# Layer C of a fused transformer kernel: softmax weights scaled and turned by one product with a diagonal, compressed keys on a block diagonal

## What is computed

```python
kc = compress(k_cmp, pe_k, wk1, wk2)          # 31 keys per group
vc = compress(v_cmp, pe_v, wv1, wv2)
# per block of 128 queries
s_c = einsum('bqghd,bngd->bghqn', qb, kc) * scale
p_c = masked_softmax(s_c, cmp_end[None, :] <= t[:, None])
o_c = einsum('bghqn,bngd->bqghd', p_c, vc)
p_s = masked_softmax(s_s, valid_s)            # selected keys
p_w = masked_softmax(s_w, valid_w)            # window keys
out = gb[..., 0:1] * o_c + gb[..., 1:2] * o_s + gb[..., 2:3] * o_w
```

## Time and profile before

| | us |
|---|---|
| median of 3 runs | 2537.54 (2537.01 to 2543.62) |
| the profiled execution, its own time | 2534.34 |
| its span in the trace | 2533.0 |
| layer C's attention in it: first logits to last values | 946.72 to 1156.83, 210.11 |
| PE busy over the span | 2307.1 (91%) |
| DVE busy | 1427.5 (56%) |
| ACT busy | 539.9 (21%) |

### The profile page before, as it was taken

The page is one execution under the profiler, slowest core; times in us unless marked ns, Lnnn a source line. Parts: engine busy times, 40 slices in busy tenths (PEclk is TensorE's granted clock), DMA queues, the critical chain, the costliest instruction groups (busy, mean ns, idle before and its releaser), DMA issues.

```text
span 2533.0 us, 29573 instructions
## 1 busy us (share of the span) xinstructions
PE 2307.1 (91%) x10920; PEld 1680.7 (66%) x10920; DVE 1427.5 (56%) x3707; ACT 539.9 (21%) x1325; POOL 65.9 (3%) x67
## 2 busy tenths in 40 slices
PE   8997889999999978889999999998889688988887
PEld 6864578888888864547888888885566533333332
DVE  6559867656656538887666566664756411111114
ACT  2013342101002015542110011103454211111111
POOL 0000000000000000000000000000000011111110
PEclk9998799999999968999999999998699899999999
DMA  5212002232224300001322223222003499999996
GB/s 206 91 50 67 1 18 84 84 93 91 84 83 153 99 18 1 1 1 51 92 92 83 83 91 93 84 84 87 1 1 135 169 357 419 419 419 419 419 420 289
DMA packets 69455, 350.18 MB, mean 138 GB/s; under 512 B 10804, under 2 KB 11060, under 8 KB 43776
## 3 DMA queue, kind: packets, MB, share of 16 engines
q1 hardware_dynamic: 64144, 339.18, 36.2%
q0 software_dynamic: 4880, 8.05, 0.9%
q10 hardware_dynamic: 288, 1.05, 0.1%
HBM read 343.05 MB, written 17.30 MB: 142 GB/s over the span
## 4 chain that ended last, share of the span: by engine, by line
PE 66%; DVE 9%; DMA 7%; ACT 3%; issue 2%; SPq 0%; DVEq 0%; POOLq 0%
PE bank L549 24%; PE bank L562 7%; PE bank L552 7%; PE bank L557 7%; PE bank L2253 6%; DMA w<-in_experts 6%; PE bank L2261 4%; PE bank L540 2%; DVE exps L1678 1%; PE bank L751 1%; DVE exps L1849 1%; PE bank L2229 1%; DMA y_pairs<-oN,idx 1%; PE bank L821 1%; PE bank L971 1%
## 5 line engine op out<-in xcount | busy, mean ns | idle before, releaser
L2253 PE MATMUL bank<-w,xT 128*64 128x512 f32 x1024 | 230.5, 598 | 9.1 <-DMA w<-in_experts 8.4
L2416 DVE COPY square<-bank 128x256 f32<-128x256 f32 x32 | 13.6, 425 | 354.3 <-ACT rope L2347 354.3
L2253 PEld LDWEIGHTS bank<-w,xT 128*64 128x64 f32 x1024 | 71.9, 138 | 162.4 <-issue 134.0
L1204 ACT ACTIVATE exps<-exps,small 128x128 f32<-128x128 f32 (+1 forms) x224 | 123.9, 554 | 183.9 <-DVE small L1678 183.9
L1449 DVE TENSOR_TENSOR third<-first,bank 128x256 f32<-128x256 f32 x108 | 45.5, 421 | 175.1 <-PE bank L549 174.4
L549 PE MATMUL bank<-u,ring 128*128 128x256 f32 x608 | 143.6, 379 | 0.0
L2261 PE MATMUL bank<-w,square 128*64 128x512 f32 x512 | 135.8, 679 | 2.1 <-ACT square L2354 2.1
L549 PEld LDWEIGHTS bank<-u,ring 128*128 128x128 f32 x608 | 115.5, 190 | 15.7
L549 PE MATMUL bank<-h_sums,w_sum 128*128 128x256 f32 x512 | 121.0, 379 | 0.0
L549 PE MATMUL bank<-h,ring 128*128 128x256 f32 x512 | 121.0, 379 | 0.0
L549 PE MATMUL bank<-u_mlp,ring 128*128 128x256 f32 x480 | 113.4, 379 | 0.0
(11 more groups left out here) (447 smaller groups left out, 4283.7 us busy)
## 6 DMA issues: line engine op xcount, KB each, us to landing
w<-in_experts SPq DMA_DIRECT2D x192, 1024.0 KB, 27.6
ring<-in_dense SPq DMA_DIRECT2D x216, 512.0 KB, 3.8
w<-y_pairs SPq DMA_DIRECT2D x4, 1024.0 KB, 26.8
consts<-in_consts SPq DMA_DIRECT2D x1, 2054.5 KB, 16.5
x<-in_xT SPq DMA_DIRECT2D x4, 512.0 KB, 7.8
cmp_v<-in_cmp_v SPq DMA_DIRECT2D x1, 2048.0 KB
cmp_k<-in_cmp_k SPq DMA_DIRECT2D x1, 2048.0 KB
h_tokens<-w SPq DMA_DIRECT2D x4, 512.0 KB, 2.9
```

The source lines that it names most:

```text
L1204: act.activation(e, e, ACT.Exp, bias=neg[:, a:a + 1], scale=-1.0, accum_out=total[:, a:a + 1]).then_inc(s[done], 1)
L2253: ins = k.pe.matmul(bank[a * CAP:(a + 1) * CAP, :], xT[:, kk % 4, kk // 4, :], w[:, (2 * (kk % 2) + a) * EH:(2 * (kk % 2) + a + 1) * EH], ...
```

## The change

Two changes in layer C's attention.

First, DVE no longer multiplies the exponentials. It forms `inv` as before, now announced by a semaphore `c_inv`. ACT makes from it, per head, a diagonal matrix of 128 by 128 (the identity times `inv` as a scale per partition, function `act_nsa_diag`), placed in its list between the exponentials of unit n and the turned copy of unit n - 3; and the transposes on PE become ordinary fp32 products of the raw exponentials with that diagonal, which scale and turn at once. The diagonals lie in 8 slots (four units of two), cut from the two tiles `square0` and `square1`, which this stage doesn't use otherwise.

Second, the compressed keys are stored on a block diagonal of 128 rows by 64 columns, so that both heads' compressed logits come from four products over all 128 rows instead of twice four over 64 rows with a semaphore between, and DVE masks them by one instruction instead of two.

```diff
+        k.diag = [sq[:, P * i:P * (i + 1)] for sq in k.sqp for i in range(4)]
-        k.kc = sb("k_cmp", [P, 32], stack=st)
+        k.kc = sb("k_cmp", [P, 2, 32], stack=st)
...
 def pe_nsa_turn(k, n):
...
         for j in range(b + 1):
-            ins = pe.transpose(k.bank[4 + a][:, j * P:(j + 1) * P], e[:, j * P:(j + 1) * P], k.const("ident"))
+            ins = pe.matmul(k.bank[4 + a][:, j * P:(j + 1) * P], e[:, j * P:(j + 1) * P], k.diag[(2 * n + a) % 8], start=True, stop=True)
...
 def pe_cmp_logits(k, m):
-    for a in range(2):
-        r = slice(a * HD, (a + 1) * HD)
-        if a:
-            pe.wait_ge(s["cmp_half"], m + 1)
-        for b in range(NB):
-            ins = pe.matmul(ch.bank[:, a * P + b * 32:a * P + (b + 1) * 32], k.yc[r, m, b * P:(b + 1) * P], k.kc[r, :],
-                            start=True, stop=True)
-        if a == 0:
-            ins.then_inc(s["cmp_half"], 1)
+    for b in range(NB):
+        ins = pe.matmul(ch.bank[:, b * 64:(b + 1) * 64], k.yc[:, m, b * P:(b + 1) * P], k.kc.rearrange("p a n -> p (a n)"),
+                        start=True, stop=True)
...
+        n = step - 2
+        if 0 <= n < len(NSA):
+            act_nsa_diag(k, n)
         n = step - 3
         if 0 <= n < len(NSA):
             act_nsa_turned(k, n)
...
+def act_nsa_diag(k, n):
+
+    act, s = k.act, k.s
+    neg, total, inv = soft_columns(k, n)
+    act.wait_ge(s["c_inv"], n + 1)
+    for a in range(2):
+        if n >= 4:
+            act.wait_ge(s["c_t_done"], 2 * (n - 4) + a + 1)
+        act.activation(k.diag[(2 * n + a) % 8], k.const("ident"), ACT.Copy, scale=inv[:, a:a + 1]).then_inc(s["c_scaled"], 1)
...
+    diagonal = own.link(dve.memset(k.kc, 0.0))
...
-    dve_take(k, k.ch6, "k_cmp", k.kc, k.ch6.bank[:, 0:32])
+    dve.wait_ge(own.sem, diagonal)
+    dve.wait_ge(k.ch6.filled, k.ch6.at["k_cmp"])
+    dve.tensor_copy(k.kc[0:HD, 0, :], k.ch6.bank[0:HD, 0:32])
+    dve.tensor_copy(k.kc[HD:P, 1, :], k.ch6.bank[HD:P, 0:32]).then_inc(k.ch6.emptied, 1)
...
 def dve_nsa_scale(k, n):
...
-    dve.wait_ge(own.sem, own.link(dve.tensor_tensor(inv, inv, k.gt[:, b, 6 * m + 1 + x:6 * m + 6:3], ALU.mult)))
-    for a in range(2):
-        e = sized_tile(k, n, b, a)
-        dve.tensor_scalar(e, e, inv[:, a:a + 1], None, ALU.mult).then_inc(s["c_scaled"], 1)
+    dve.tensor_tensor(inv, inv, k.gt[:, b, 6 * m + 1 + x:6 * m + 6:3], ALU.mult).then_inc(s["c_inv"], 1)
...
 def dve_cmp_logits(k, m):
-    for a in range(2):
-        ins = dve.scalar_tensor_tensor(pc[:, a::2, :], k.ch7.bank[:, a * P:(a + 1) * P].rearrange("p (b n) -> p b n", n=32), SCALE,
-                                       add[:, :, a, :], ALU.mult, ALU.add)
-    ins.then_inc(k.ch7.emptied, 1)
+    dve.scalar_tensor_tensor(pc.rearrange("p a n -> p (a n)"), k.ch7.bank[:, 0:2 * P], SCALE, k.const("cmp_add"),
+                             ALU.mult, ALU.add).then_inc(k.ch7.emptied, 1)
```

More of the change, by code:

```diff
@@ L290, in signals @@
     s.new("lg_done", "masked", "exp_done", "t_done", "turned0", "turned1")
-    s.new("c_lg_done", "c_masked", "c_exp_done", "c_scaled", "c_t_done", "c_turned0", "c_turned1", "c_weighed")
+    s.new("c_lg_done", "c_masked", "c_exp_done", "c_scaled", "c_inv", "c_t_done", "c_turned0", "c_turned1", "c_weighed")
     s.new("gates_exp", "cmp_k_in", "cmp_v_in", "cmp_2_in", "win_zero")
-    s.new("win_v", "win_k", "hid_z", "hid_exp", "hid_ready", "cmp_half", "cmp_shifted", "cmp_exp", "cmp_weights")
+    s.new("win_v", "win_k", "hid_z", "hid_exp", "hid_ready", "cmp_shifted", "cmp_exp", "cmp_weights")
     s.new("zeroed", "row_out", "bias_in", "lam_dot", "lam_exp", "qk_normed")
@@ L829, in pe_cmp_logits @@
 def pe_cmp_logits(k, m):
-    pe, s, ch = k.pe, k.s, k.ch7
+    pe, ch = k.pe, k.ch7
     pe.wait_ge(ch.emptied, ch.n)
-    for a in range(2):
-        r = slice(a * HD, (a + 1) * HD)
-        if a:
-            pe.wait_ge(s["cmp_half"], m + 1)
-        for b in range(NB):
-            ins = pe.matmul(ch.bank[:, a * P + b * 32:a * P + (b + 1) * 32], k.yc[r, m, b * P:(b + 1) * P], k.kc[r, :],
-                            start=True, stop=True)
-        if a == 0:
-            ins.then_inc(s["cmp_half"], 1)
+    for b in range(NB):
+        ins = pe.matmul(ch.bank[:, b * 64:(b + 1) * 64], k.yc[:, m, b * P:(b + 1) * P], k.kc.rearrange("p a n -> p (a n)"),
+                        start=True, stop=True)
     ch.end(ins, ("cmp", m))
@@ L1868, in dve_cmp_logits @@
     mx, sm = cmp_columns(k, m)
-    add = k.const("cmp_add").rearrange("p (b a n) -> p b a n", a=2, n=32)
     dve.wait_ge(k.ch7.filled, k.ch7.at["cmp", m])
-    for a in range(2):
-        ins = dve.scalar_tensor_tensor(pc[:, a::2, :], k.ch7.bank[:, a * P:(a + 1) * P].rearrange("p (b n) -> p b n", n=32), SCALE,
-                                       add[:, :, a, :], ALU.mult, ALU.add)
-    ins.then_inc(k.ch7.emptied, 1)
+    dve.scalar_tensor_tensor(pc.rearrange("p a n -> p (a n)"), k.ch7.bank[:, 0:2 * P], SCALE, k.const("cmp_add"),
+                             ALU.mult, ALU.add).then_inc(k.ch7.emptied, 1)
     dve.wait_ge(k.ch7.emptied, k.ch7.at["cmp", m])
```

## The result

| | before | changed |
|---|---|---|
| median, 7 runs each | 2537.01 us | 2547.70 us |
| ratio, with its 95% interval | | 1.0042 (1.0024 to 1.0061) |
| span of the profiled execution | 2533.0 | 2551.6 |
| layer C's attention in it | 210.11 | 219.42 |

A forecast was written before the change was run, and what follows sets the result against it. DVE paced the old stage; afterwards PE's queue of 23.1 us plus 3.4 of waits gives 26.5 a round. Rounds and drain add 11.1, the clock takes 2.5: net +8.5 on 2537.5, 2546 us, range 2531 to 2556.

The forecast's parts named there:

- The doubled products: PE's turns: an fp32 product takes two records of 0.11 us against a transpose's one, 4.4 us more a round.
- The compressed logits: On PE: 8 records instead of 16 and a stop, 0.9 us instead of 2.10, 1.1 less a round.
- The walk through a round: Following one round's waits: PE's queue of 23.1 us plus 3.4 of waits makes 26.5, against 25.4 before.
- steps 1 and 4: Places in a round where PE waits for ACT's copy of bank 4, put at 1.46 and 1.17 us.
- The terms of the sum: Layer C's attention: first round +0.6, six rounds +6.6, last round 1.1, drain 2.0 and 0.8, clock -2.5; net +8.5 us.
- the drain: Behind the last logits, three units turn with nothing beside them: 2.0 us, and their diagonals some 0.8.
- A fall's price: In the old kernel's rounds, 3.6 us at half clock cost 0.5 us: 25.94 instead of 25.43.
- the rival of the dearer clock: Falls stay while PE bounds, 1.8 us instead of 0.5 per 3.6 us fall: 2554 us, slower, chance 0.11.
- The clock's term: Later half-clock falls in the stage mostly go as PE's queue gets fuller: -2.5 us.
- PE's queue alone: Rival: the waits of PE close, rounds of 23.5 us, 2525 us, faster; chance 0.15 together with cheap products.
- Cheap products: Rival: one record per product, rounds of 23.6 us, 2523 us, faster; chance 0.15 together with PE's queue alone.
- A cancelled loss: Rival: ACT's diagonals at 0.20 instead of 0.30 us, rounds of 25.9, 2541 us, same; chance 0.16.

The follow-up runs named there:

- the keys alone: The kernel before with only the block-diagonal compressed keys and the single masking instruction; DVE still scales, PE still transposes: 0.9968 of before, stage 200.45 us.
- the second pair: The kernel before and the changed kernel, each profiled a second time unchanged: stage 211.2 us and 220.4 us.

## Why the prediction was right, and where its sizes were off

- **What bounded before**: DVE. Shown by the keys alone, where DVE's work stays, its wait goes, and the round is shorter by that wait.
- **The diagonal's length**, priced at 0.39 long and 0.30 from start to start from the scalings at the program's start: 0.387, and the pair before the copy 0.59 (1011.50 to 1012.09).
- **The doubled products**, 0.11 a record: sixteen in 2.05. Right; and 640 records stand in the stage.
- **The compressed logits** within 1.05 us: 1.10 with the modelled tail, the next product 0.95 behind the first.
- **The walk through a round**: the waits of steps 1 and 4 are there, both for ACT's copy. Measured from the round's first logits at 1008.24 the three-block turn begins at 4.34 (4.32 forecast) and the two-block turn of step 4 at 14.41 (14.33). The waits themselves read smaller, 1.23 and 0.99 for 1.46 and 1.17, because the view counts a product's modelled tail of some 0.2 as busy. The round: 26.60 for 26.5.
- **The terms of the sum.** They add up to 8.6, which the prediction gives as 8.5; the stage measured +9.3. Counting rounds from one compressed logits to the next, the six middle ones went from 154.2 to 159.6, +5.4. At full clock a round grew by 1.17, 7.0 for six, where 6.6 was put; the falls of the old kernel had cost these rounds 1.6, which is gone. The last and the drain went from 30.8 to 34.3, +3.5, which holds what the old kernel's last fall had cost too, where +3.9 was put. The first went from 24.60 to 24.77, +0.2 where +0.6 was put, but this term can't be judged by one pair: in the second pair it went from 24.84 to 25.76, +0.9, since the clock stood at half for 6.8 us of it in both. The step from the first logits to the compressed ones adds 0.2. The second pair gives +4.6 for the middle and +9.2 in all.
- **DVE's busy time in a round**: the prediction has 18.6 in one place and "under 18" in another. Measured are 18.82 in a round with the input sums and 17.40 in one without, 18.1 in the mean. Nothing hangs on it, since DVE is no bound in either.
- **A fall's price.** The old kernel's middle rounds with a fall, 25.93 for 25.43, are also those with the input sums. That the fall makes the difference was not certain from the earlier trace rows; with the keys alone both kinds of round last 24.5, and in the old kernel's rounds with a fall DVE waits 0.40 us for logits inside it, at a place where the other rounds have no wait. So it does. For a round that PE paces the rival of the dearer clock put 1.8 us on 3.6 at half clock; in the kernel with the diagonals and the old keys 6.8 us at half clock cost 2.4, which is less.
- **The clock's term came out right by luck.** No fall came behind the first 17 us of the stage in either profile of the changed kernel, as assumed. But the prediction gave the fuller queue of PE as the reason, and the kernel with the keys alone has an emptier one (PE busy for 80% of the windows above, where the kernel before has 83) and no falls either, while the kernel with the fullest, 91%, has one. The Trainium skill ("TensorE: Matmul & The Clock Gate", "Part 4: PE-mode transpose") says that a transpose doesn't count as activity the way a product does. The transposes put back into the changed kernel, which brought three falls, fit that; the keys alone don't, since this kernel turns by transposes and ran at 1.00 twice, with nothing changed against before but the compressed keys.

The rivals: PE's queue alone (rounds of 23.5) would have needed the waits to close. Cheap products fell by 640 records. A cancelled loss would have needed diagonals at 0.20. A dearer clock would have needed falls in the stage. The sign of 1.1 us a round was near enough to zero that swapping two steps of ACT's list took most of it away, and this was not among my rivals: they changed prices, not the order.

## What to carry to other kernels

Moving work off the engine that paces a pipelined loop helps only as far as the receiving engines' places in the loop allow. Here 4.8 us a round left DVE, which set the pace, 4.4 came to PE and 4.6 to ACT, both of which had idle time, and the round got longer. Two things did it, which overlap and don't add: the products that took the place of transposes (26.60 against 24.22 without them), and the diagonals ahead of the copy that frees bank 4, of which there is one (26.60 against 25.91 with the copy first). The first is the larger: even with the copy first the diagonals lose. Put new work behind the step that others wait for, price what the new form costs the engine that is second in line, and look at a change of two parts by halves: the gain of one hid in the loss of the other. An fp32 product in place of a transpose is twice the records.

## What the runs showed of the hardware

The granted clock of this stage goes with the kernel and its falls come at nearly the same places in two executions: with the old kernel the later falls start 54.8, 106.0, 157.2 and 184.5 us behind the stage's first logits in one execution, and 55.9, 107.1, 158.3 and 185.6 us in the other, which has one more at 28.6. The keys alone, which take 1.1 us of products and a wait of DVE of about 0.9 us out of each round of 25.4, made all of these vanish, though PE is then busy for a smaller share; a stretch of 6.8 us at half clock near the stage's start stayed.
